# The boundary between the two layers: where the context row is summed and how often the engines meet

## The reference, cut to what matters

```python
def ec_moe(h, router, w1, w3, w2):
    ...
    hid = jax.nn.silu(jnp.einsum('becd,edf->becf', xs, w1)) * jnp.einsum('becd,edf->becf', xs, w3)
    out = jnp.einsum('becf,efd->becd', hid, w2) * gate[..., None].astype(h.dtype)
    return jnp.zeros_like(h).at[bidx, idx].add(out)
...
            h = layer_norm(DN_ALPHA * h + g2 * ec_moe(u, moe_router[l], moe_w1[l], moe_w3[l], moe_w2[l]),
                           ln_g[l, 1], ln_b[l, 1])
```

## Time and profile before

| | us |
|---|---|
| median of 3 runs | 4100.66 |
| lowest, highest | 4098.81, 4101.08 |
| the profiled execution | 4103.48 |
| its span | 4101.7 |
| last expert of layer 0 done on PE | about 2169.0 |
| next stage begins | about 2182.55 |

### The profile page before, as it was taken

One profiled execution on the slowest core, in us unless ns is written; L12 is line 12 of the kernel. 1 busy time (PEld: TensorE's weight loads), 2 busy tenths in 40 slices (PEclk: granted clock), 3 DMA queues, 4 the chain that ended last, 5 costly groups with the idle time before them and its releaser, 6 DMA issues. The chain is left out here.

```text
span 4101.7 us, 64264 instructions
## 1 busy us (share of the span) xinstructions
PE 3954.2 (96%) x27921; PEld 3452.7 (84%) x27921; DVE 1442.0 (35%) x3193; ACT 675.6 (16%) x1658; POOL 475.7 (12%) x401
## 2 busy tenths in 40 slices
PE   7999999899799999999998999999979999999999
PEld 4767775564599999999997888886469999999998
DVE  6444456675502121110005666565640000000004
ACT  0122321104210101110104111111411111110101
POOL 0000002343400000000005111010330000000000
PEclk9999999999799999999999999999989999999999
DMA  8410002233578888877784011104247777877776
GB/s 328 181 33 29 28 17 70 71 116 122 208 292 296 313 297 313 300 272 278 272 289 156 30 38 53 37 28 177 86 179 282 272 282 272 326 271 282 274 281 242
DMA packets 143458, 788.99 MB, mean 192 GB/s; under 512 B 14840, under 2 KB 46248, under 8 KB 97098
## 3 DMA queue, kind: packets, MB, share of 16 engines
q1 hardware_dynamic: 133818, 750.80, 49.1%
q0 software_dynamic: 9360, 34.08, 3.9%
HBM read 725.10 MB, written 59.74 MB: 191 GB/s over the span
## 5 line engine op out<-in xcount | busy, mean ns | idle before, releaser
L2564 PE MATMUL PS<-arena 128*128 128x144 f32 x11264 | 1440.4, 286 | 2.5 <-ACT arena L766 2.3
L2564 PEld LDWEIGHTS PS<-arena 128*128 128x128 f32 x11264 | 1405.5, 190 | 3.7 <-ACT arena L766 2.8
L2715 DVE TENSOR_TENSOR arena<-PS,arena 128x144 f32<-128x144 f32 x352 | 108.3, 308 | 1859.9 <-ACT arena L2651 1859.8
L2541 PE MATMUL PS<-arena 128*128 128x144 f32 x5632 | 742.7, 286 | 0.0
L2541 PEld LDWEIGHTS PS<-arena 128*128 128x128 f32 x5632 | 711.4, 190 | 1.6 <-DVE arena L2715 1.6
L2651 ACT ACTIVATE arena<-PS 128x144 f32<-128x144 f32 x352 | 102.1, 290 | 1697.0 <-PE PS L2564 1697.0
L3205 PE MATMUL PS<-arena 128*128 128x256 f32 x1568 | 344.2, 379 | 0.0
L3205 PEld LDWEIGHTS PS<-arena 128*128 128x128 f32 x1568 | 295.3, 190 | 38.7
L2480 POOL DMA_INDIRECT expert_sum<-arena x31 | 51.0, 1646 | 2006.0 <-DVE arena L2634 2006.0
L2080 PE MATMUL PS<-arena 128*128 128x512 f32 x576 | 258.7, 598 | 2.4 <-PEq L3791 1.9
L2080 PEld LDWEIGHTS PS<-arena 128*128 128x128 f32 x576 | 105.3, 190 | 119.2 <-issue 118.3
(11 more groups left out here) (444 smaller groups left out, 3576.3 us busy)
## 6 DMA issues: line engine op xcount, KB each, us to landing
arena<-expert_panels SPq DMA_DIRECT2D x352, 1536.0 KB, 6.7
arena<-ada_w SPq DMA_DIRECT2D x6, 4096.0 KB, 16.3
arena<-ada_w SPq DMA_DIRECT2D x12, 2048.0 KB, 11.9
arena<-odd_w_in SPq DMA_DIRECT2D x16, 1024.0 KB, 6.2
arena<-hgrn_w SPq DMA_DIRECT2D x20, 512.0 KB, 3.9
arena<-filter_spectra SPq DMA_DIRECT2D x36, 256.0 KB, 2.8
mid_rows<-arena SPq DMA_DIRECT2D x18, 512.0 KB, 2.9
filter_spectra<-arena SPq DMA_DIRECT2D x16, 512.0 KB, 4.0
```

Of the source, the lines that this page charges most:

```text
L2541: m = pe.matmul(PS[:, m_ // 3, m_ % 3 * SLOTS:m_ % 3 * SLOTS + SLOTS], s.w2[n % s.ring][:, m_ * P:(m_ + 1) * P], s.hid[:, f, :], start=f = ...
L2564: m = pe.matmul(PS[:, 6 + n % 2, q * 256:q * 256 + SLOTS], s.w13[n % s.ring][:, q, k, :], s.xs[e % 2][:, k, :], start=k == 0, stop=k == KD ...
L2715: dve.tensor_tensor(s.hid[:, f, :], PS[:, 6 + n % 2, 256:256 + SLOTS], s.sil[n % 2], ALU.mult).then_inc(s.hd, 1)
```

## The change

It has four parts.

1. In layer 0 the first half of the context sum is done in the ninth expert too. `sum_first_ctx` (two calls of 128 x 512) runs at step 5 in both layers; at step 6 DVE multiplies both halves of the columns by the gate row and then adds the residual into a new buffer `part`. The wait for `ym` ahead of the turn of step 7 now holds in both layers.
2. The second half, with `outc[1]`, leaves the expert stage. `sum_ctx` is now two calls, issued by PE as the first work of the next stage (`LayerInput.sum_ctx`); DVE's first work there is `end_ctx`: two multiplications of 128 x 512 and one addition of `part` of 128 x 1024, each linked by a wait, and then the statistics of tile 0 as before.
3. SP, behind the loads of row tiles 1 to 5, waits for the end of that (`cy`) before it issues the constants, since they overwrite what the sum reads.
4. Behind the last stage of each of the three blocks `stage_end` becomes a plain `drain()` on each engine, with no semaphore; the two other meetings stay.

```diff
             def sum_ctx(s, pe):
 
-                pe.wait_ge(s.ce, 2)
                 for n in range(2):
-                    for half in range(2):
-                        m = pe.matmul(PS[:, n, :], s.hot_t[:, half, :], s.outc[half][:, n * 512:(n + 1) * 512],
-                                      start=half == 0, stop=half == 1)
-                m.then_inc(s.yf, 1)
+                    m = pe.matmul(PS[:, n, :], s.hot_t[:, 1, :], s.outc[1][:, n * 512:(n + 1) * 512], start=True, stop=True)
+                return m
+
+            def end_ctx(s, dve, ch):
+
+                for n in range(2):
+                    hs = slice(n * 512, (n + 1) * 512)
+                    m = dve.tensor_tensor(s.yc[:, hs], PS[:, n, :], s.g2[:, 1, hs], ALU.mult)
+                ch.link(m)
+                m = dve.tensor_tensor(s.yc, s.yc, s.part, ALU.add)
+                ch.link(m)
...
-                        if f == 5 and e == 8 and s.ending:
+                        if f == 5 and e == 8:
                             s.sum_first_ctx(pe)
...
                 s.turn_ctx(pe, 1, 6)
-                s.sum_ctx(pe)
...
-                        if s.ending and e == 8 and f == 6:
+                        if e == 8 and f == 6:
                             dve.wait_ge(s.yf, 1)
                             for n in range(2):
...
+                                    m = dve.tensor_tensor(s.part[:, hs], PS[:, 3 + n, :], s.g2[:, 1, hs], ALU.mult)
+                                m.then_inc(s.ym, 1)
+                            if not s.ending:
+                                dve.wait_ge(s.ym, 2)
+                                ch.link(dve.tensor_tensor(s.part, s.part, s.res_ctx, ALU.add))
...
-                dve.wait_ge(s.yf, 1)
-                for n in range(2):
-                    m = dve.tensor_tensor(s.yc[:, n * 512:(n + 1) * 512], PS[:, n, :], s.g2[:, 1, n * 512:(n + 1) * 512], ALU.mult)
-                ch.link(m)
-                dve.tensor_tensor(s.yc, s.yc, s.res_ctx, ALU.add)
...
+            def sum_ctx(s, pe):
+                s.experts.sum_ctx(pe).then_inc(s.cf, 1)
+
+            def end_ctx(s, dve, ch):
+                dve.wait_ge(s.cf, 1)
+                s.experts.end_ctx(dve, ch)
+                dve.engine_nop().then_inc(s.cy, 1)
...
                 s.feed.sync_first(sp)
+                sp.wait_ge(s.feed.cy, 1)
...
                 f = s.feed
+                f.sum_ctx(pe)
                 f.turn(pe, 0)
...
                 f = s.feed
+                f.end_ctx(dve, ch)
                 f.stats(dve, ch, 0)
...
                 s.pe(pe)
-                stage_end(pe, "pe")
+                if s is not stages[-1]:
+                    stage_end(pe, "pe")
+                else:
+                    pe.drain()
```

More of the change, by code:

```diff
@@ L2382, in build, with __init__ @@
         class Experts:
-            def __init__(s, l, pick, base, g2, xsc, res_ctx, yc, beside, preload, more=(), ending=None, g2c=None):
+            def __init__(s, l, pick, base, g2, xsc, res_ctx, yc, beside, preload, more=(), ending=None, g2c=None, part=None):
                 s.l, s.beside, s.preload, s.ending = l, beside, preload, ending
+                s.part = at(yc if ending else part, D)
                 if ending:
@@ L2591, in pe @@
                                 pe.wait_ge(s.ce, 1)
-                                if s.ending:
-                                    pe.wait_ge(s.ym, 2)
+                                pe.wait_ge(s.ym, 2)
                             s.turn_rows(pe, e + 1)
@@ L2731, in dve @@
                             ch.link(dve.tensor_copy(s.g2c.rearrange("p a b -> p (a b)"), PS[:, 5, 0:2 * KD]))
-                        if s.ending and e == 8 and f == 6:
+                        if e == 8 and f == 6:
                             dve.wait_ge(s.yf, 1)
                             for n in range(2):
-                                dve.tensor_tensor(s.yc[:, n * 512:(n + 1) * 512], PS[:, 3 + n, :],
-                                                  s.res_ctx[:, n * 512:(n + 1) * 512], ALU.add).then_inc(s.ym, 1)
+                                hs = slice(n * 512, (n + 1) * 512)
+                                if s.ending:
+                                    m = dve.tensor_tensor(s.part[:, hs], PS[:, 3 + n, :], s.res_ctx[:, hs], ALU.add)
+                                else:
[4 more added lines that the diff above has]
+                                ch.link(dve.tensor_tensor(s.part, s.part, s.res_ctx, ALU.add))
                         if s.ending and e == E_N - 1:
@@ L2869, in build, with __init__ @@
             TILES = [NL] + list(range(NL))
-            def __init__(s, l, uT, scratch, yc, cols, scattered):
-                s.l, s.uT, s.scattered = l, uT, scattered
+            def __init__(s, l, uT, scratch, experts, cols, scattered):
+                s.l, s.uT, s.experts, s.scattered = l, uT, experts, scattered
                 s.st = [at(scratch + 24 * b, 24) for b in range(3)]
                 s.tmp, s.early = at(scratch + 72, KD, 2), at(scratch + 96, 1)
-                s.x = [yc] + [at(scratch + 1024 + b * D, D) for b in range(1, 4)] + [at(16384 + b * D, D) for b in range(2)]
+                s.x = [experts.yc] + [at(scratch + 1024 + b * D, D) for b in range(1, 4)] + [at(16384 + b * D, D) for b in range(2)]
                 s.ln = at(scratch + 5120, 2, D)
@@ L2882, in __init__ @@
                 s.tx, s.ua, s.ud = sm("turned"), sm("u_act"), sm("u_dve")
+                s.cf, s.cy = sm("ctx_sum"), sm("ctx_row")
                 s.hm, s.ho, s.hs = sm("row_gained"), sm("row_done"), [sm(f"row_stored{b}") for b in range(2)]
@@ L3778, in build @@
         next_block()
-        mixer1 = Retention(uT1, yT1, 18432, wts1, ring, LayerInput(1, uT1, 23040, experts0.yc, first_cols, indirect[0][2]))
+        mixer1 = Retention(uT1, yT1, 18432, wts1, ring, LayerInput(1, uT1, 23040, experts0, first_cols, indirect[0][2]))
         end1 = LayerEnd(1, 14592, 2048, 26880, 41472, last_rows)
@@ L3801, in _ @@
                 s.sync(sp)
-                stage_end(sp, "sp")
+                if s is not stages[-1]:
+                    stage_end(sp, "sp")
+                else:
+                    sp.drain()
         @block.gpsimd
@@ L3808, in _ @@
                     s.pool(pool)
-                stage_end(pool, "pool")
+                if s is not stages[-1]:
+                    stage_end(pool, "pool")
+                else:
+                    pool.drain()
         @block.tensor
@@ L3821, in _ @@
                 s.act(act, ch)
-                stage_end(act, "act")
+                if s is not stages[-1]:
+                    stage_end(act, "act")
+                else:
+                    act.drain()
         @block.vector
@@ L3828, in _ @@
                 s.dve(dve, ch)
-                stage_end(dve, "dve")
+                if s is not stages[-1]:
+                    stage_end(dve, "dve")
+                else:
+                    dve.drain()
 OUTS = {"y_prompt": (1, L_CTX, D), "y_sample": (1, L_LAT, D),
```

2 lines of the change are left out of this document (1 added, 1 removed).

## The result

The changed kernel takes 4107.2 us (median of 20 executions, 4102.8 to 4109.34) against 4099.64 us of the kernel before beside it (20, 4097.86 to 4103.2). The ratio is 1.0017, 95% interval 1.0010 to 1.0023: slower by 7.56 us, between 4 and 9.4. Forecast was +7.7 us, within 0.2% of no change.

The account below looks back on a forecast made before the run. PE, busy 96% of the span, was taken as the bound, with POOL's drain last at the layer boundary. Ninth expert +1.71, meetings -0.45 and head +6.4 gave +7.7 us: 4108.4 us on the median, range 4104.8 to 4110.4.

Parts of the forecast that it names:

- The drain: Boundary between the layers: POOL's drain ends last, by 0.8 us, because it waits for its scatter DMA to land.
- The first rival: POOL's drain waits only for the scatter's issue, so the next stage begins earlier: 4100.7 to 4102.5 us; chance 5%.
- The ninth expert: Layer 0, step 5: two added calls on a PE that never waits cost +1.7 us; DVE's extra work costs nothing.
- The old tail: Behind the last expert: removed calls and DVE operations give nothing back, since they ended before POOL's drain.
- One meeting less: Block ends: dropping the semaphore meeting saves about 0.45 us in sum, bounds 0 and 0.9; 0.3 at the layer boundary.
- The new head: Next stage's start: PE's half sum at 1.2 GHz (3.8 us) and DVE's part (2.63) precede the statistics, +6.4 us.
- The fourth rival: The clock returns later than before, slowing the first products; slower by over 0.2%, 4109 to 4110.5 us; chance 36%.
- The third rival: The head's sum wakes the clock early, so turns and first products run at 2.4 GHz, 3.4 us back: 4105.0; chance 9%.
- The second rival: The head's sum runs at 2.4 GHz: +5.9 us, 4106.5; chance 4%.
- The sum: Whole kernel: +1.71 - 0.45 + 6.4 = +7.7 us, giving 4108.4 us on the median, slower by 0.19%.
- SP's wait: Next stage: constants, norm rows and a weight piece start up to 3.9 us later, at zero cost.

Follow-up runs that it names:

- e9: Changed kernel with layer 0's last scatter writing its rows instead of adding them; 4103.99 us against 4099.23 for the kernel before.
- e4: Changed kernel without layer 0's last scatter, row loads waiting for fifteen; 4102.17 us against 4099.56 for the kernel before.
- e8: Changed kernel with POOL waiting for the semaphore of layer 0's last scatter before draining; 4108.49 us against 4099.23 for the kernel before.
- e2: Kernel before with the sum's first half in layer 0's ninth expert, second half and meetings as they were; 4102.09 us against 4099.56.
- e1: Kernel before with a plain drain replacing the semaphore meeting behind each block's last stage; 4098.81 us against 4099.56.
- e3: Changed kernel with the head undone: the sum's second half again behind the last expert; 4101.97 us against 4099.56 for the kernel before.
- e10: Changed kernel with layer 0's last scatter moved to POOL's first instruction of the next stage; 4099.44 us against 4099.23 for the kernel before.
- e7: Kernel before with SP made to wait for tile 0's norm before issuing its constants; 4098.98 us against 4099.25.
- e5: Kernel before with one meeting less, plus unread products: three behind the context sum, three before turn 0, two between turns; 4092.32 us against 4099.25.
- e6: Changed kernel plus unread products: nine behind the context rows' turn, six behind the sum, two between turns; 4098.72 us against 4099.25 for the kernel before.
- e11: Changed kernel with the last scatter in the next stage, plus unread products (1, 6 and 2); 4095.11 us against 4099.23 for the kernel before.
- e12: Kernel before with one meeting less and eight short unread products behind the context sum, none in the next stage; 4094.53 us against 4099.74.

## Why the prediction was right

**The drain**: right, and it carries the forecast. The gap to the landing was 1.3 us in after and 1.4 in e9 with a shorter flight. The first rival, that the drain waits for the issue only, is refuted by after and e9. But "POOL's drain waits for its DMA" was half of the truth. The first part of the drain's 2.6 us hides beside the flight, and only e4 and e8 could show it, since in rows 3 and 4 the landing came later than that part both times. The mistake was harmless for the forecast and cost 2.1 us in e4's expectation.

**The ninth expert**: +1.71 forecast, 1.71 on PE's timeline, 1.4 in the stage's length. No cost of DVE's work shows.

**The old tail**: nothing back, as e2 and after show.

**One meeting less**: -0.45 forecast. The stage came 0.34 sooner at the boundary, with -0.3 forecast. The end of the first block was a miss, as a term of the sum: "no more than a hop is saved, under 0.1". PE's first work of the second block, in before and in after (timelines):

```profile
908.18 1.10 PE L2080 MATMUL PS<-arena 128*128 128x512 f32 x2 [1.89 <-PEq L3791]
```

```profile
907.88 1.53 PE L2080 MATMUL PS<-arena 128*128 128x512 f32 x3 [1.56 <-PEq L3809]
```

PE's gap is 1.56 instead of 1.89, 0.33 less: here the engine that came last to a meeting still paid 0.33 for its own semaphore and branch. At the kernel's end the stretch from SP's drain to the end shrank by 0.2. Together -0.9, the bound that was given; e1's median, -0.75, is too uncertain to confirm it.

**The new head**: +6.4 forecast, 6.39 measured at turn 0 and 6.38 at turn 1 against before, with PE's sum 3.75 for 3.8 and DVE's part with its hops 2.63 for 2.63. "Nothing covers it" holds against before, less so against e3, where the row load was late and the head cost 5.06 at turn 1. The fourth rival had the clock come back later. In the profile of after it came 3.1 us behind the start of turn 1 instead of 4.6, and turn 2 is 0.75 nearer to turn 1 for it. This isn't the head's doing: among the kernels with the head and no unread products the clock came back 2.7 us (e8), 3.1 (after), 3.6 (e10), 5.5 (e4) and 5.6 (e9) behind turn 1, among those without the head 3.1 (e7) to 4.8 (e2). The rival's cost exists, then, at half a microsecond for each microsecond of lateness, as scatter between executions; the 4.6 that the forecast started from was one draw of it.

The third rival, that the sum would wake the clock in time for the turns, didn't come true: the clock rose at 2182.2, was gone by 2185.6, and turn 0 started at 2187.98, 2.4 us later. The Trainium skill, TensorE: Matmul & The Clock Gate, "What's actually happening", says that activity releases the throttle; the trace agrees, but in after the rise came 0.6 us behind the end of that activity, in e4 0.35 ahead of it. The second rival, the sum at 2.4 GHz, is refuted by the 3.75 us: in after the clock fell at 2171.9, 4.1 us behind PE's last product.

**The sum** from the profiles, taken at turn 1, ahead of the clock's scatter: turn 1 comes 14.99 - 8.61 = 6.38 later behind the stage and the stage 0.34 sooner, the ninth expert is +1.4 to +1.7, the first block's and the kernel's end -0.5. That is +6.9 to +7.3. The medians say +7.6, with 4 to 9.4, so they fit but can't test any single term. That 7.56 lies 0.1 from 7.7 is luck: the meetings were off by 0.4, and the interval is 5 us wide. The end of the two profiles says less still: in the profile of after PE also waits 1.9 us less for the state stores (3.1 for 5.0), which no part of the change is known to cause, and that with the 5.7 us ahead of the first silu makes its span 0.7 us the shorter.

**SP's wait**: zero. e7 shows it for 1.4 us of lateness; for the 4.0 us of the changed kernel (3.9 forecast) after shows POOL's start only 0.28 later behind the stage and no new wait.

## What to carry to other kernels

Before moving work from one side of a meeting to the other, read which engine's drain ends last. What ended earlier was free where it stood here, and was paid nearly in full on the other side. Work put first behind a meeting can run at the low clock after a long wait: here the half sum took 3.75 us behind 9.9 us without PE work, where 1.71 were paid beside other products.

If the last drain is POOL's and holds an indirect DMA, try the DMA behind the meeting (e10, stage 7.3 us sooner), and look at once at who reads what it writes.

Compare two profiles place by place, since their ends can differ the other way than the medians do. Before a difference at one place is put down to the change, look at the same place in a run whose edit doesn't touch it: e7 shows that the 0.75 us which the clock seems to give back in after come and go without the change.

## What the runs showed of the hardware

- POOL's drain took 2.59 us (e4) and 2.67 us (e8) with no DMA of POOL under way, and ended 1.3 to 1.4 us behind the landing where one was.
- The same turns and products got the 2.4 GHz clock back 2.7 to 5.6 us behind the start of turn 1, in one profile each of eleven kernels: 1.4 us between the shortest and the longest stretch.
- The clock can fall although PE is working again. In e5 PE's gap was 2.44 us, in e6 1.90, both between 128x512 products, and it fell 1.3 and 0.4 us after PE had resumed, and was back only at 2183.8 and 2184.7. In e11 PE's gap was 1.78 us and the clock stayed at 1.00. A window of e6 from the low stretch:

```profile
2182.00:2183.00 1.00, 1.00 (x2) 0.34 (x1) 0.00 (x0) 0.41 (x2) 0.00 (x0) 0.50 0.76 279
```

- With eight unread products of PE in one stage DVE's waits for the state stores of three heads, some 160 to 480 us later, came to 7.8 us instead of 11.5 (e12, e1). The cause is open. A change of a tenth of a per cent can be of this kind, with nothing of it at the place that was changed.
